# Second feed-forward on one Trainium2 core: the narrow column group moved from last to first, and the output projection begun in halves of four column groups

## The reference, cut to what matters

```python
def _conv_ffn(h, w_in, conv_w, conv_b, w_out):
    gate, up = jnp.split(h @ w_in, 2, axis=-1)
    return (jax.nn.silu(_dwconv(gate, conv_w, conv_b)) * up) @ w_out
...
x = _layer_norm(ALPHA * x + ml[2] * yl, ln_g[i, 0], ln_b[i, 0])
f = _conv_ffn(_modulate(x, ml[3], ml[4]), ffn_w_in[i], ffn_conv_w[i], ffn_conv_b[i], ffn_w_out[i])
x = _layer_norm(ALPHA * x + ml[5] * f, ln_g[i, 1], ln_b[i, 1])
```

## Time and profile before

| | us |
|---|---|
| median of three runs | 2256.47 (2254.18 to 2256.76) |
| profiled execution, its time | 2256.98 |
| profiled execution, its span | 2255.1 |
| PE busy in the span | 2185.1 |
| second feed-forward, first matmul of group 0 | at 2039.95 |
| first matmul behind the last idle gap of that stage | at 2175.86 |

### The profile page before, as it was taken

The page is one execution under the profiler, slowest core; times in us unless marked ns, Lnnn a source line. Parts: engine busy times, 40 slices in busy tenths (PEclk is TensorE's granted clock), DMA queues, the critical chain, the costliest instruction groups (busy, mean ns, idle before and its releaser), DMA issues.

```text
span 2255.1 us, 33501 instructions
## 1 busy us (share of the span) xinstructions
PE 2185.1 (97%) x13484; PEld 1813.9 (80%) x13484; DVE 1340.2 (59%) x2204; ACT 1182.5 (52%) x2002; POOL 0.2 (0%) x4
## 2 busy tenths in 40 slices
PE   8989999989999999999999999999999998999998
PEld 8769989949999777887677677868888877669998
DVE  5776645785655665445666665366666336546764
ACT  4666534575544664444344443366655337447764
POOL 0000000000000000000000000000000000000000
PEclk9999999999999999999999999999999999999999
DMA  8744575754576222222122221222222222214542
GB/s 310 284 143 176 223 300 196 282 199 149 187 298 246 108 76 92 94 94 93 57 75 75 75 75 56 94 75 94 94 94 94 102 86 94 94 59 150 185 169 94
DMA packets 45719, 312.28 MB, mean 138 GB/s; under 512 B 4951, under 2 KB 7255, under 8 KB 8580
## 3 DMA queue, kind: packets, MB, share of 16 engines
q1 hardware_dynamic: 45572, 310.20, 37.9%
HBM read 309.11 MB, written 1.07 MB: 138 GB/s over the span
## 4 chain that ended last, share of the span: by engine, by line
PE 84%; DVE 9%; ACT 5%; issue 1%; DMA 0%; ACTq 0%; DVEq 0%; SPq 0%
PE bank L801 63%; PE bank L806 8%; DVE ws L1838 2%; ACT ws L1343 2%; PE bank L1207 2%; PE bank L996 1%; DVE xs L1863 1%; PE bank L1178 1%; DVE hT L1994 1%; PE bank L1291 1%; PE bank L1140 1%; DVE arena L2267 1%; PE bank L1273 1%; ACT xs L1367 1%; PE bank L824 1%
## 5 line engine op out<-in xcount | busy, mean ns | idle before, releaser
L801 PE MATMUL bank<-xs,ws 128*128 128x256 f32 (+1 forms) x9600 | 1559.7, 323 | 26.1 <-DVE xs L1863 16.1
L801 PEld LDWEIGHTS bank<-xs,ws 128*128 128x128 f32 x9600 | 1388.7, 190 | 202.3 <-issue 32.5
L1838 DVE TENSOR_TENSOR ws<-ring,ws 128x1024 fp32r<-128x1024 f32 x462 | 545.5, 1222 | 292.4 <-ACT ws L1343 292.2
L1343 ACT ACTIVATE ws<-ring 128x1024 fp32r<-128x1024 f32 x462 | 462.8, 1050 | 301.7 <-PE bank L801 201.8
L1863 DVE TENSOR_TENSOR xs<-arena,xs 128x512 fp32r<-128x512 f32 (+1 forms) x286 | 162.3, 581 | 290.8 <-ACT xs L1367 289.3
L1367 ACT ACTIVATE xs<-arena 128x512 fp32r<-128x512 f32 (+1 forms) x286 | 149.3, 539 | 317.7 <-PE bank L801 212.8
L806 PE MATMUL bank<-ws,xs 128*128 128x512 f32 (+1 forms) x1008 | 229.5, 387 | 3.8 <-DVE xs L1863 2.9
L1863 DVE TENSOR_TENSOR xs<-hT,xs 128x512 fp32r<-128x512 f32 (+1 forms) x216 | 133.4, 619 | 153.5 <-ACT xs L1367 153.4
L1367 ACT ACTIVATE xs<-hT 128x512 fp32r<-128x512 f32 (+1 forms) x216 | 122.9, 573 | 193.9 <-PE bank L801 184.9
L806 PEld LDWEIGHTS bank<-ws,xs 128*128 128x128 f32 x1008 | 187.2, 188 | 44.2 <-DVE xs L1863 5.1
L1860 DVE SCALAR_TENSOR_TENSOR xs<-xT,par,xs 128x256 fp32r<-128x256 f32 x112 | 51.1, 479 | 11.8 <-ACT xs L1365 11.8
(11 more groups left out here) (265 smaller groups left out, 1378.8 us busy)
## 6 DMA issues: line engine op xcount, KB each, us to landing
ring<-in_stream SPq DMA_DIRECT2D x232, 1024.0 KB, 4.8
arena<-in_side SPq DMA_DIRECT2D x57, 1024.0 KB, 5.0
arena<-bias_vectors SPq DMA_DIRECT2D x1, 1536.0 KB, 9.0
hT<-in_tokens SPq DMA_DIRECT2D x1, 1024.0 KB, 5.4
arena<-in_tokens SPq DMA_DIRECT2D x1, 1024.0 KB, 13.0
out<-arena SPq DMA_DIRECT2D x2, 512.0 KB, 3.1
arena<-in_params SPq DMA_DIRECT2D x1, 918.0 KB, 8.5
arena<-bias_vectors SPq DMA_DIRECT2D x1, 706.0 KB, 10.5
```

What stands on the lines that cost most here:

```text
L801: ins = mm(ps(n, c, c + g.T), a[wi][:, p * P:(p + 1) * P], x[xi], start=first, stop=last)
L1343: do(ws[:, i % 2, 0, c], ring[:, w % R, c], ACT.Copy).then_inc(w_high, 2 // halves_in)
L1838: ins = v.tensor_tensor(ws[:, i % 2, 1, c], ring[:, w % R, c], ws[:, i % 2, 0, c].bitcast(F32), ALU.subtract)
```

## The change

`ffn_in` of layer 1 gets its narrow group first (group 0) and five wide ones behind it; inner blocks are numbered by `ffn_at`. `ffn_out` of layer 1 begins with three chunks in two passes: tickets 0 to 3 for chunks 0, 1 and 2, then tickets 4 to 7 for the same chunks (each then counted as done), and from chunk 3 on in the old order. The last group is now a wide one with four pairs; on ACT their taps stand one behind each of the chunks 0 to 3 of `ffn_out`, and ACT doesn't go ahead to the next weight slot behind chunk 3. DVE's code only takes the new numbering. The first feed-forward and the mixer's output projection `m_out` compute as before (`piece` replaces `out_piece`).

```diff
+def ffn_at(l, i):
+    return max(4 * i - 2, 0) if l else 2 * i
...
     for i in range(6):
-        w.group(("ffn_in", 1, i), 8 if i < 5 else 4, KD, T, "h", fresh=None if i else 3, pair=True)
+        w.group(("ffn_in", 1, i), 8 if i else 4, KD, T, "h", fresh=None if i else 3, pair=True)
...
     for i in range(6):
-        n.add(("ffn_in", 1, i), 4 if i < 5 else 2)
+        n.add(("ffn_in", 1, i), 4 if i else 2)
...
+            def piece(g, p, k):
+
+                n, cols = N(g.name, p), SLOT // g.kc
+                if k == 0:
+                    pe.wait_ge(bank_free[n % BANKS], n // BANKS)
+                a = [ws[:, (g.s0 + k // g.kc) % 2, j, k % g.kc * cols + p * P:k % g.kc * cols + p * P + P] for j in range(2)]
+                x = [split_x(g.q0 + k, j) for j in range(2)]
+                mm(ps(n, 0, g.T), a[0], x[0], start=k == 0, stop=False)
+                mm(ps(n, 0, g.T), a[0], x[1], start=False, stop=False)
+                return mm(ps(n, 0, g.T), a[1], x[0], start=False, stop=False)
...
-                summed_linear(("ffn_out", l), 2 * l + 1, (0, LAT)[l])
+                if l == 0:
+                    summed_linear(("ffn_out", l), 1, 0)
+                    return
+
+                g = G("ffn_out", 1)
+                for p0 in (0, 4):
+                    for k in range(3):
+                        pe.wait_ge(slot_done, g.w0 + k // g.kc + 1)
+                        pe.wait_ge(x_done, g.q0 + k + 1)
+                        for p in range(p0, p0 + 4):
+                            ins = piece(g, p, k)
+                        if p0:
+                            ins.then_inc(chunk_done, 1)
+                linear(g, 3, g.K - 2)
+                summed_tail(g, 3, LAT)
...
-                        feed_to(nxt.q0 + k)
+
+                        feed_to(nxt.q0 + k, not (l and last and k == 3))
                         for p in range(before):
-                            if k != start + 2 * p // before:
+                            if k != start + (p if l and last else 2 * p // before):
                                 continue
-                            j = per * (i - 1) + p
+                            j = ffn_at(l, i - 1) + p
```

More of the change, by code:

```diff
@@ L1211, in _ @@
             out_ = G("m_out")
[L1213 to L1221, removed]
             pe.wait_ge(slot_done, out_.w0 + 1)
@@ L1225, in _ @@
             for p in range(KD - 1):
-                out_piece(p, 0)
+                piece(out_, p, 0)
             seen(sq_ready, MH - 1)
@@ L1231, in _ @@
                 if p == 4:
-                    out_piece(KD - 1, 0).then_inc(chunk_done, 1)
-                ins = out_piece(p, 1)
+                    piece(out_, KD - 1, 0).then_inc(chunk_done, 1)
+                ins = piece(out_, p, 1)
             ins.then_inc(chunk_done, 1)
@@ L1700, in ffn @@
             def ffn(l, lo):
-                groups, per = ((NFF // 2, 2), (6, 4))[l]
+                groups = (NFF // 2, 6)[l]
                 for i in range(groups + 1):
@@ L1729, in ffn @@
                         if start + 2 <= k < start + 2 + before:
-                            j = per * (i - 1) + k - start - 2
+                            j = ffn_at(l, i - 1) + k - start - 2
                             c = ctmp[:, j % 4, lo:]
@@ L2591, in pack_stream @@
         pairs = [f[:, P * (j + NFF * i):P * (j + NFF * i + 1)] for j in range(NFF) for i in range(2)]
-        per = (4, 8)[l]
-        for i in range(-(-2 * NFF // per)):
-            group(("ffn_in", l, i), *pairs[per * i:per * (i + 1)])
+        for i in range((NFF // 2, 6)[l]):
+            group(("ffn_in", l, i), *pairs[2 * ffn_at(l, i):2 * ffn_at(l, i + 1)])
         group(("ffn_out", l), np.asarray(x["ffn_w_out_2"][l]))
```

## The result

| | before | changed |
|---|---|---|
| median of 20 runs, us | 2254.12 (2253.51 to 2256.76) | 2258.20 (2256.49 to 2259.83) |
| profiled execution, us | 2256.98 | 2257.90 |
| span of it, us | 2255.1 | 2255.8 |

The ratio is 1.0016, 95% interval 1.001 to 1.0022: 0.16% slower. The interval leaves out 1, so the difference is real; it lies within the 0.2% that the forecast called no change. The forecast was 2258.9 with a range of 2254.5 to 2261.3. The kernel before had shown 2256.47 over three runs and has 2254.12 over twenty, so the distance is 4.1 us between medians (3.7 between means) where the forecast had 2.4. The profile says where the first 2.6 of it lie.

A forecast was written before the change was run, and what follows sets the result against it. PE was busy 97% of the span, leaving 6.45 us of losses to aim at. Waits of 4.14 + 2.02 + 0.95 = 7.11 against 4.70, clock loss unchanged, gave 2256.47 + 2.41 = 2258.9 us, range 2254.5 to 2261.3.

The forecast's parts named there:

- Start, 4.14: Narrow group 0: PE waits 0.71, 1.80 and 1.58 for chunks 1, 2 and 6, and 0.05 at group 1.
- the third term: Group 0, chunk 6: ready late behind the third weight slot's split, 1.58 us lost.
- Chunk 2 of the output projection, 2.02: Start of ffn_out: chunk 2 ready 4.90 behind the last wide group, first pass covers 2.88, 2.02 us lost.
- Bank waits gone: ffn_out's last tickets of the first chunk: the 1.29 us wait for ACT's bank copy goes.
- Third slot, 0.95: ffn_out, chunk 4: its slot waits for chunk 1, multiplied only in the second pass; 0.95 us lost.
- Waits in all, 2.41 slower: Second feed-forward: PE waits sum to 7.11 us against 4.70 before, so 2.41 us slower.
- I let it cost the same 1.75: Behind the 2.02 gap in ffn_out: the clock falls as behind the former 1.98 gap, costing 1.75 us again.
- The base: Whole kernel before the change: 2256.47 us, to which the forecast added 2.41.
- the clock falls in group 0 too: Rival, group 0's early gaps: one fall costs up to 1.75 us, giving 2260.2; chance 0.18 for once.
- The halves do what they say: Rival, ffn_out: chunk 2 ready within the first pass, no 2.02 and no clock loss, 2255.1 us; chance 0.05.
- the start is hidden: Rival, group 0: the layer norm feeds narrow chunks in time, 4.72 us lost, 2254.7 us; chance 0.03.
- Both: Rival, start and end of the feed-forward: all 6.45 us of losses gone, 2250.0 us; chance 0.03.

The follow-up runs named there:

- e7: Changed kernel, second weight slot of group 0 split early, mostly inside the layer norm, third slot behind chunk 7: 2255.35 us, ratio 1.0002 to the kernel before.
- e6: Changed kernel, with the third weight slot split behind chunk 7 and not chunk 5 of group 0: 2255.47 us, ratio 1.0007 to the kernel before.
- e3: Changed kernel, DVE's taps one chunk later behind the last wide group, third slot split only when chunk 4 needs it: 2255.96 us, 1.0004 to before.
- e5: Changed kernel, output projection begun with tickets 0 to 5 for chunks 0 and 1, then 6 and 7; ACT's order as before: 2252.71 us, ratio 0.9993.
- e1: Changed kernel with the narrow group first but the output projection begun the old way, without halves: 2255.45 us, ratio 0.9998 to the kernel before.
- e2: Changed kernel with the halves only, the narrow group staying last as before: 2257.68 us, ratio 1.0009 to the kernel before.
- e8: Changed kernel with e7's early slot and e5's six-and-two beginning together: 2250.79 us, ratio 0.9978 to the kernel before.
- e11: The kernel before, run again unchanged in a later series: 2254.26 us, ratio 0.9997 to the kernel before in that series.
- e12: The changed kernel, run again unchanged in a later series: 2258.08 us, ratio 1.0017 to the kernel before in that series.

## Why the prediction was right, and where it was short

- **Start, 4.14.** Shown: 0.72 + 1.78 + 1.65 = 4.15, at the chunks named. e7 took the slot splits away from between the chunks and 1.2 remained; e6 took away the third term alone.
- **Chunk 2 of the output projection, 2.02.** Shown: 2.19 start to start. That DVE's taps in front of it make 0.9 of it is shown by e3 (1.30 left, start to start), that the short cover is the cause by e5 (0).
- **Bank waits gone.** Shown; e1 brings 1.08 and 0.58 back without the halves.
- **Third slot, 0.95.** Shown: 0.97 as the idle gap reads, 1.18 start to start where the clock held. It did not come in e2 and e3, where no taps stand between the slot's split and chunk 4.
- **Waits in all, 2.41 slower.** Shown: 2.6 in the traces. The median of e8 moved as its waits did (3.7 less, with 3.5 less of waiting). Those of e5 and e7 lie 1.3 and 1.2 from what their waits give, which is more than their waits changed; alone they show nothing.
- **"I let it cost the same 1.75": the clock.** The cost of a fall was right (1.69), but it is not one number for every execution. The fall behind a gap of about 2 us came in the profiled executions of before, e11 (both 1.98), e2 (1.98 and 2.40), the changed kernel and e7, not in those of e6 and e12 (2.08 and 2.07). The medians of the first series lie 4.1 apart and those of e12 and its series 2.8, the means 3.7 and 3.4, where the waits give 2.6. Part of the rest is the clock: the mean granted clock over the 109 executions of the kernel before beside the experiments and in e11 is 0.9979, over the 31 of the changed kernel 0.99765. Of 2256 us that is 0.6, with a standard error of 0.4. Filling the gap moved both kernels by like amounts. So that the changed kernel loses somewhat more clock is likely but not shown, and where it would fall more often stays open.
- **The base.** 2256.47 over three runs was 2.3 above the 2254.12 over twenty. The forecast of 2258.9 was so near 2258.20 by two errors that cancel, which is luck: a base too high by 2.3 and a difference too small by 1.7.
- **The rivals.** That the clock falls in group 0 too was seen in none of the traces with the gaps of 0.72 and 1.78 side by side. "The halves do what they say" and "the start is hidden" fell with the gaps seen. "Both" was reckoned wrongly: by the forecast's own terms the 0.95 would have stayed, which gives 2251.0 and not 2250.0.

On the clock the Trainium skill, "TensorE: Matmul & The Clock Gate", Part 1, says that the place of its change varies between runs of one kernel. The traces agree, and here even whether it changes varies: behind the same gap of 2.07 the changed kernel kept 1.00 in one execution and had 0.50 in another. The 109 ns that follow for 256 columns from its section "Back-to-back issue gap" are by that section the gap of isolated matmuls. With a weight load to each matmul 984 of them took 118.40 us, 120 ns each, also in the changed kernel.

## What to carry to other kernels

When PE works in shorter steps, ask for every prepared operand how much PE work lies between its release and its use, and compare with the whole queue that the preparing engine has in between, not with the preparation alone: here the 4.9 to 5.1 us of ACT and DVE queue behind a released slot were covered by 5.77 us of matmuls, and halves or narrow groups give 2.88 to 4.33. If banks come free late, split the work unevenly so that the first pass ends where they come free (six and two tickets), and keep the number of matmuls per weight slot. Work whose inputs lie ready, as a weight slot, can go into idle stretches of the stage in front.

## What the runs showed of the hardware that was not expected

- A product of plain float32 operands (128 x 128 by 256 columns) took 0.44 us as two matmul records; each matmul of the split operands took 0.12.
- Behind an idle gap of about 2.0 us TensorE's granted clock fell to 0.50 in some executions and stayed at 1.00 in others of the same kernel: it fell behind six of the eight gaps of 1.98 to 2.40 traced. Behind gaps of 1.54 and less in this stage it fell in none of the traces here. A fall cost 1.7 us in this stage (1.69 and 1.75).
- One kernel's executions on one chip fell into groups by mean granted clock (0.999 and 0.997), some 2 to 3 us apart.
- Two high halves of a weight slot on ACT and one low half on DVE, put into the layer norm's gaps (e7), did not widen the gap in front of group 0: 0.54, with 0.57 before. The gap in front of the statistics' four matmuls grew from 0.50 to 0.58.
